# Prompt attention of three branches: one phase, two heads in step, values on column halves

## The reference

```python
h = einsum('bsd,de->bse', x, w_in)              # q, k, v of each branch, ..., gates (3 * 1024 columns)
# A: causal, logits + F[t] - F[s]; B: window of 128 with learned sinks, 2 key heads for 8 heads;
# C: keys of 96, causal by chunks of 64
s = einsum('bqhd,bkhd->bhqk', q, k);  s = where(mask, s, -inf)
o = einsum('bhqk,bkhd->bqhd', softmax(s), v)    # B: the sink joins the sum of the softmax
br_n = o_n * silu(gate_n)                       # stored as br_n
merged = sum_n sigmoid(g_n) * (br_n @ w_br_n);  y = merged @ w_o
```

## Time and profile before

| | us |
|---|---|
| median of 3 runs | 3792.36 (3791.45 to 3795.2) |
| the profiled execution | 3789.74 |
| its span, first to last instruction | 3788.1 |
| PE busy in the span | 3390.3 (89%), 20866 matmuls |
| DVE, ACT, POOL busy | 1411.7, 885.1, 125.5 |
| mean granted clock of TensorE | 0.952 of full speed |

### The profile page before, as it was taken

One profiled execution on the slowest core, in us unless ns is written; L12 is line 12 of the kernel. 1 busy time (PEld: TensorE's weight loads), 2 busy tenths in 40 slices (PEclk: granted clock), 3 DMA queues, 4 the chain that ended last, 5 costly groups with the idle time before them and its releaser, 6 DMA issues. The chain is left out here.

```text
span 3788.1 us, 54850 instructions
## 1 busy us (share of the span) xinstructions
PE 3390.3 (89%) x20866; PEld 2834.0 (75%) x20866; DVE 1411.7 (37%) x3261; ACT 885.1 (23%) x1982; POOL 125.5 (3%) x64
## 2 busy tenths in 40 slices
PE   0999978998998997989969999789989999978988
PEld 0888865887997885667758888568879878855877
DVE  5114233333343332354631233334333333323556
ACT  1221212332222332220221112123322233322110
POOL 0000000100100000000000000000000001000000
PEclk9999988999999998989979999889999989988999
DMA  5322225221433225753442222342233243186533
GB/s 194 106 89 94 77 89 160 62 64 39 108 76 98 59 72 142 244 220 126 144 153 92 88 91 67 120 123 64 64 74 91 60 98 87 37 231 212 218 129 107
DMA packets 485460, 423.06 MB, mean 112 GB/s; under 512 B 300452, under 2 KB 394532, under 8 KB 482916
## 3 DMA queue, kind: packets, MB, share of 16 engines
q1 hardware_dynamic: 451444, 381.06, 33.7%
q10 hardware_dynamic: 33840, 39.66, 3.2%
HBM read 295.36 MB, written 127.64 MB: 112 GB/s over the span
## 5 line engine op out<-in xcount | busy, mean ns | idle before, releaser
L351 PE MATMUL proj_acc<-proj_wh,keep_xh 128*128 128x512 f32 (+1 forms) x1296 | 502.1, 387 | 12.5 <-DVE proj_wl L326 12.5
L352 PE MATMUL proj_acc<-proj_wl,keep_xh 128*128 128x512 f32 (+1 forms) x1296 | 500.8, 386 | 0.0
L353 PE MATMUL proj_acc<-proj_wh,keep_xl 128*128 128x512 f32 (+1 forms) x1296 | 500.7, 386 | 0.0
L351 PEld LDWEIGHTS proj_acc<-proj_wh,keep_xh 128*128 128x128 f32 x1296 | 244.5, 189 | 58.4 <-DVE proj_wl L326 13.3
L352 PEld LDWEIGHTS proj_acc<-proj_wl,keep_xh 128*128 128x128 f32 x1296 | 244.6, 189 | 45.7
L353 PEld LDWEIGHTS proj_acc<-proj_wh,keep_xl 128*128 128x128 f32 x1296 | 244.4, 189 | 45.7
L1820 PE MATMUL up_acc<-up_wh,up_bh 128*128 128x512 f32 x432 | 173.1, 401 | 12.8 <-DVE up_wl L1864 12.8
L326 DVE TENSOR_TENSOR proj_wl<-proj_raw,proj_wh 128x512 fp32r<-128x512 f32 (+1 forms) x144 | 96.1, 676 | 210.6 <-ACT proj_wh L321 210.6
L1056 PE MATMUL att_c_gacc<-att_c_gwh,keep_xh 128*128 (+1 forms) x576 | 170.7, 296 | 2.9 <-DVE att_c_gwl L1185 2.9
L1056 PE MATMUL att_b_gacc<-att_b_gwh,keep_xh 128*128 (+1 forms) x576 | 170.7, 296 | 2.3 <-DVE att_b_gwl L1185 2.3
L1056 PE MATMUL att_a_gacc<-att_a_gwh,keep_xh 128*128 (+1 forms) x576 | 169.9, 295 | 1.9 <-DVE att_a_gwl L1185 1.9
(11 more groups left out here) (338 smaller groups left out, 6803.6 us busy)
## 6 DMA issues: line engine op xcount, KB each, us to landing
up_gates<-scratch_gates SPq DMA_DIRECT2D x18, 1536.0 KB, 8.3
proj_raw<-in_w_in SPq DMA_DIRECT2D x48, 512.0 KB, 3.8
str_ka<-in_cache_a_kT SPq DMA_DIRECT2D x16, 1024.0 KB, 9.0
str_va<-in_cache_a_v SPq DMA_DIRECT2D x16, 1024.0 KB, 5.3
scratch_sg<-proj_out SPq DMA_DIRECT2D x54, 256.0 KB, 2.1
up_br<-scratch_br SPq DMA_DIRECT2D x54, 256.0 KB, 8.2
scratch_gates<-att_a_gout SPq DMA_DIRECT2D x24, 384.0 KB, 2.6
scratch_gates<-att_b_gout SPq DMA_DIRECT2D x24, 384.0 KB, 2.7
```

The costliest lines, as they stand in the source:

```text
L351: nc.tensor.matmul(bank, hi, wh[:, u, kt, 0:w], start=kt == 0, stop=False)
L352: nc.tensor.matmul(bank, hi, wl[:, u, kt, 0:w], start=False, stop=False)
L353: mm = nc.tensor.matmul(bank, lo, wh[:, u, kt, 0:w], start=False, stop=kt == KT - 1)
```

## The change

Three calls become one, `prompt_attention(nc, C, T, S, l)`, and the loop over pairs is written out: twelve units (kind, pair) in one list. A unit has 16 sub-steps m; the row tile is a = m // 2 and the head m % 2, so two heads go in step. Sub-step m holds turn m, score m+2 (or the first two of the next unit), on even m a `back`, a fill if m is 0 to 8, from m = 3 on (not 5) one preparation of the next unit, on odd m the values of both heads. What is new in the operations:

- q and k are kept as a high and a low part in fp32r. ScalarE copies a transposed group as the high part, VectorE subtracts it from the same bank as the low part, and only then is the bank free. A score is three fp32r matmuls a chunk of 512.
- Kind a's extra row: F only goes to k; kind b's sink is no longer a matmul, VectorE copies it behind the score into PSUM. Kind b's two heads share one prepared k.
- Values: v (64 columns of a head) is the weight, on one half of the array's columns, and `pt` is moving; the heads' results stand on partition halves of `oo`. VectorE copies them to `ot`, TensorE transposes back (`back`), and VectorE scales and gates both halves.
- The gate weights have one buffer in two halves; GpSimd splits all of them, after the last fill of the unit before. Rows of q and k have two buffers, a head's half each.

```diff
+    fills = [0, 1, 2, 3, 4, 5, 6, 7, 8]
...
+        for m in range(SUBS):
+            order.append(("turn", n, m))
+            if m + 2 < SUBS:
+                order.append(("score", n, m + 2))
...
+            if m in fills:
+                order.append(("fill", n, fills.index(m)))
+            if ahead and m >= 3 and m != 5:
+                order.append(("prep", n + 1, *ahead.pop(0)))
+            if m % 2:
+                order.append(("value", n, m // 2))
...
-                    last = c + cw == w
-                    nc.tensor.matmul(ss[:, s, c:c + cw], lhs, kt[:, u, first + c:first + c + cw],
-                                     start=True, stop=not last)
+                    nc.tensor.matmul(bank, hi, khi, start=True, stop=False)
+                    nc.tensor.matmul(bank, hi, klo, start=False, stop=False)
+                    nc.tensor.matmul(bank, lo, khi, start=False, stop=c + cw < w)
...
-                        for j, t in enumerate(tiles(a)):
-                            mm = nc.tensor.matmul(oo[:, 0:HD], pt[:, s, j * P:(j + 1) * P], v[:, u, t, :],
-                                                  start=j == 0, stop=j == len(tiles(a)) - 1)
+                for j, t in enumerate(tiles):
+                    for u in range(2):
+                        half = slice(u * HD, u * HD + HD)
+                        mm = nc.tensor.matmul(oo[half, 0:P], v[:, n % 2, t, slice(0, HD) if kind == "b" else half],
+                                              pt[:, u, j * P:(j + 1) * P], start=j == 0, stop=j == len(tiles) - 1,
+                                              skip_group_check=True, tile_position=(0, u * HD))
...
+            def back(n, a):
+                g = groups["back", n, a][0]
+                pe.wait_ge(ot_ready, PT * n + a + 1)
+                bank_free(pe, g)
+                nc.tensor.transpose(tr[:, g % 2, 0:P], ot[:, a % 2, :], C["ident"][:]).then_inc(tr_made, 1)
...
+            def prep(n, x, u, half):
+                g = groups["prep", n, x, u, half][0]
+                act.wait_ge(tr_made, g + 1)
+                nc.scalar.activation(prepared((qh, kh), n, x, u, half), tr[0:ROWS[UNITS[n][0]], g % 2, :], ACT.Copy)\
+                    .then_inc(hi_made, 1)
...
+            def prep(n, x, u, half):
+                g = groups["prep", n, x, u, half][0]
+                if x == "k" and half == 0 and UNITS[n][0] == "a":
+                    extra(n, u)
+                dve.wait_ge(hi_made, preps[n, x, u, half] + 1)
+                nc.vector.tensor_tensor(prepared((ql_, kl_), n, x, u, half), tr[0:ROWS[UNITS[n][0]], g % 2, :],
+                                        prepared((qh, kh), n, x, u, half).bitcast(F32), ALU.subtract)\
+                    .then_inc(tr_taken[g % 2], 1)
...
+                    pool.wait_ge(gw_loaded, 16 * (2 * n + half + 1))
+                    if n:
+                        pool.wait_ge(g_made, NT * n)
```

More of the change, by code:

```diff
@@ L1082, in _, with prepared @@
+            for what, *of in order:
+                {"prep": prep, "score": score, "turn": turn, "value": value, "back": back, "fill": fill}[what](*of)
+        def prepared(tiles, n, x, u, half):
+            return tiles["qk".index(x)][0:ROWS[UNITS[n][0]], n % 2, u, 512 * half:512 * half + 512]
         @block.scalar
         def _(act):
[L1084 to L1092 removed]
@@ L1190, in prompt_attention, with groups_all @@
+            dve.wait_ge(sink_loaded, 16)
+            for what, *of in order:
+                if what == "prep":
+                    prep(*of)
+                elif what == "score":
+                    highest(*of)
+                elif what == "turn":
+                    turn(*of)
+                elif what == "value":
+                    value(*of)
+                elif what == "back":
+                    back(*of)
     ph.end()
+def groups_all(groups):
+    return [g for gs in groups.values() for g in gs]
```

608 lines of the change are left out of this document (276 added, 332 removed).

## The result

| | before | changed |
|---|---|---|
| median, range (us) | 3791.67, 3787.88 to 3795.20 (5 runs) | 3818.11, 3808.94 to 3829.06 (5 runs) |
| ratio to before | | 1.0067 (95%: 1.0051 to 1.0083) |
| profiled execution, span (us) | 3789.74, 3788.1 | 3829.06, 3827.4 |
| mean granted clock | 0.952 | 0.932 |
| attention, layer 1 and 2 (us, first to last matmul) | 820.6, 820.7 | 830.5, 836.5 |

The change makes the kernel 0.7% slower; 3742 was forecast, and the time lies outside the range.

The account below looks back on a forecast made before the run. TensorE was taken to bound the attention stage, busy 778.85 of 826.05 us. Pairs and starts gain 36 us a layer, 72 in all, less 24 for the clock: net 48, so 3742 us, range 3680 to 3805.

Parts of the forecast that it names:

- the round through the two-engine copy: Fill-free sub-steps: softmax, ScalarE copy, VectorE subtraction, next turn take 5.25 us; waits 9.5 us a pair (A, C), 5.5 (B).
- The clock: Fill-free sub-steps: TensorE's clock falls in every second pair, 12 falls at 2 us each, 24 us lost.
- A's extra row: A's second key waits for the row VectorE writes late, part of the chain, 1 us beyond it.
- Rival 2: Short clock falls in every pair: 24 falls at 3 us, 72 us instead of 24; 3790, no change; chance 0.13.
- B's pairs: Branch B: TensorE's work 44.8 us plus 5.5 of waits, 50.3 us a pair against 51.6 before.
- A's and C's clean pairs: Branches A and C: TensorE's work 61.6 us plus 9.5 of waits, 71.1 us a pair against 71.6 before.
- rival 5: Values: the two column halves don't overlap, 0.448 us a tile, 96 us more in all; 3838; chance 0.04.
- rivals 1 and 4: Fill-free waits: shorter, 6 and 3 us a pair (3690, chance 0.20), or longer, 14 and 8 (3834, chance 0.08).
- The start: Start of a layer's attention: three phases become one, about 24 us to first turn; 20 us outside pairs instead of 47.
- Rival 3: Sub-steps 9 to 15: clock stays low throughout, 11 us more a pair in A and C; 3910; chance 0.09.
- The three marks of the last section: Signs of being wrong: A's pair below 68 or above 74, clock 0.5 beyond 10 us between pairs, waits for gate weights.
- The likeliest case: The prediction's own case for the whole kernel: net gain 48 us, 3742, own range 3715 to 3770, chance 0.46.

Follow-up runs that it names:

- e7: The changed kernel with the nine fills of A and C in sub-steps 0, 1, 2, 3, 5, 6, 7, 9 and 10; 3801.13 us, ratio 1.0013.
- e6: The changed kernel plus matmuls nobody reads: eight in sub-steps 9 to 13 of A and C, five ahead of B's later values; 3795.75 us, ratio 1.0006.
- e12: The changed kernel with B's queries and keys taken to 65 rows instead of 64, the keys' 65th row zero; 3792.58 us, ratio 0.9986.
- e13: e11 with B's queries and keys taken to 65 rows instead of 64; 3655.65 us, ratio 0.9642.
- e10: e3 with the value products in the form of the kernel before the change and no transposes back; 3841.96 us, ratio 1.0122.
- e2: The changed kernel with the next unit's preparations in sub-steps 1 to 8 instead of 3, 4 and 6 to 11; 3708.65 us, ratio 0.9782.
- e3: The changed kernel with the next unit's preparations in sub-steps 0 to 7, ahead of the back and the fill; 3695.68 us, ratio 0.9752.
- e11: e3 with each transpose back issued one sub-step later, in the odd ones, ahead of the values there; 3669.33 us, ratio 0.9676.

## Why the prediction was wrong

The wait that I took for the main one, the round through the two-engine copy, was right, and so was its size. What failed are the terms around it. The forecast's span was 3740.4; the profile has 3827.4, 87 us more:

1. **The clock, a term mis-sized, and with it A's extra row**: "I take one fall in every second pair, 12, at 2 us each ... 24 us". Against clean pairs (72.1, which e7 shows for A as well; 53.0, the last of B 55.7 by e6) the pairs of the two layers are 25 and 32 us too long: 56, so +32. A's first three pairs hold 31 of it, B's and C's 25. Falls stand in 14 of 24 pairs, and such a pair is up to 9 us longer. In A not all of this is the clock: the prediction had the wait for the extra row as "part of the chain, 1 us beyond it", and it is 2.9 us, 17.6 in six places, since the row is held until GpSimd's subtraction ends. e6 keeps this wait and cuts these falls to 3.4 us; its six pairs of A are still 19 us too long, 12 less than here, and of the 25 us in B and C nothing is left but its own products. So the falls cost 12 + 25 = 37 us at least, where 24 was charged. The other 19, the wait with a fall of 3.4 us behind it, I can't split exactly: at half the clock six falls of 3.4 us can lose 10 us at most, so 9 or more are the wait's. Rival 2 was thus half true. The row to see the falls by stood in the prediction; I gave the swing a price per fall from no row, and read the mean of 0.97, which belongs to an order with fills at both ends of a pair, as if it spoke for one without.
2. **B's pairs, a term mis-sized**: "B 44.8 + 5.5 = 50.3". 53.0 was measured, and 55.7 for the last, of which some 0.8 can be e6's own products: (3 x 2.7 + 5.4) x 2 = 27. I charged the switch of TensorE's form for the values and not for B's 64-row scores. e12 gives 2.1 of the 2.7 back.
3. **The stream attention, a term left out**: unchanged code, 15.7 us more. The clock is low at its beginning, as before the change, and falls again 27 and 44 us later; the first and the last of these stretches, in windows whose columns are as above:

```profile
1484.00:1500.00 16.00, 8.66 (x30) 5.88 (x31) 2.54 (x6) 2.27 (x4) 1.50 (x2) 0.57 1.16 248
...
1528.00:1538.20 10.20, 10.16 (x33) 7.04 (x33) 1.40 (x6) 1.74 (x5) 0.00 (x0) 0.52 0.93 309
```

   In e6 it takes 141.3 and 137.4, in e13 136.3 and 144.9, so it varies by itself, and I can give only part of these 15.7 to the change. What it varies with shows over both stream attentions of all fifteen kernels, from 134.6 to 148.8 us: a straight line through them is 125.1 us and 0.47 for each us at the lower level (21 to 50 us by the clock rows; correlation 0.92). Here that is 82 us low against 55 before, so 13 of the 15.7.
4. **A's and C's clean pairs**: 72.1 for 71.1, seven a layer, 14. The first fp32r product behind transposes in fp32 starts its successor 0.31 to 0.33 us later, not 0.227 (1318.19 to 1318.52 in the timeline); 16 x 0.09 = 1.4 a pair, of which waits hide some.

32 + 27 + 15.7 + 14 = 89, two more than the 87.

Point by point, what held. *Values*: passes of a pair of halves start a median of 0.109 us apart, 20 records in 1.31 us; 0.218 a tile is confirmed, and with it rival 5 falls. *Fp32r of 128 columns*: 0.112 to 0.117, taken 0.115. *The round*: 5.30 for 5.25, with waits of 1.07, 1.11 and 1.29 where 1 to 2 were named, so rivals 1 and 4 fall as the prediction had them; in A one wait of 2.9 lies outside that. *The nine sub-steps with fills*: in C's pair at 1265.16 the first wait for a bank is that at 1307.9, behind the last fill. *Gate weights*: no wait for them anywhere; behind the last fill of B's first pair GpSimd is done 11.1 us later (1020.12 against 1008.98), for a bound of 13, and the next fill comes after 14.3. *The start*:

```profile
643.54 1.97 PE L987 MATMUL att_tr<-keep_ident,att_row 128*65 128x128 f32 x8 [9.56 <-DMA att_row<-scratch_qa]
651.77 1.94 PE L987 MATMUL att_tr<-keep_ident,att_row 128*65 128x128 f32 x8 [6.26 <-DVE att_row L1116]
659.67 1.97 PE L987 MATMUL att_tr<-keep_ident,att_row 128*65 128x128 f32 x8 [5.96 <-DMA att_row<-scratch_qa]
...
667.57 0.47 PE L1020 MATMUL att_tr<-keep_ident,att_p 128*128 128x128 f32 x1
```

The first load is issued at 640.24, so the first turn, at 667.57, comes 27.3 us behind it, where 24 was forecast. ("Where it was 14" is a misreading: in the kernel before the first turn stands at 650.87, 11.2 us behind the first load; at 14 is the first gate matmul.) From the first load to the last matmul some 21 us lie outside the pairs, when the clean ones and what they are too long by are taken off; 20 was forecast, so the gain of the starts came. *Rival 3* (low through the whole stretch) did not come in C; A comes near it only with the old values (e10). The three marks of the last section: A's pair is above 74, the clock is low for 13.7 us between pairs, and TensorE doesn't wait for the gates' weights. Two of three said that I was wrong.

The chances: 0.21 for slower, of which no case named the right sum. The likeliest case was right about the waits but for A's extra row, and wrong about the engine's speed. The deeper error is of order: I took where the preparations stand as given and asked what it costs, but did not ask what else the same chain does, which is to make TensorE's queue thin just where nothing dense follows.

## What to carry to other kernels

A copy out of PSUM that needs two engines in turn belongs beside dense work of TensorE; the same instructions, moved by a few sub-steps, were worth 109 to 122 us (e2, e3), four times what the whole change lost. Where TensorE waits and the profile names no releaser, look in the code for what it waits for, and at that operation's own length: here 0.17 us had become 1.5. When a change takes work off TensorE in a stretch that already waits, charge the granted clock of that stretch and of the stage behind it as terms of their own. Count the rows of every operand against 64 before and after: e11 with 65 rows (e13) is the best version found, 3655.65 us, 3.6% below the kernel before.

## What was not expected of the hardware

- An operand of 64 rows, with no tile asked for, costs 0.175 us going in from full-width transposes and 0.086 us coming out; 65 rows cost nothing of it (e12, e13).
- The first fp32r product of 512 columns behind plain fp32 work takes 0.31 to 0.33 us to its successor, the next 0.23.
- The clock can stay low for 30.7 us with TensorE busy 30.39 of them (e10), so a full queue of instructions alone did not bring it back at once.
- VectorE's extra row (128x8 from SBUF to SBUF) takes 0.17 us alone. In the six places where GpSimd's subtraction (128x1024) was under way it took 1.33 to 1.68 and ended 0.03 us behind it, while VectorE's maximum over PSUM, begun at 799.13 beside GpSimd's cast and the start of its subtraction, took its usual 1.09. Why the one is held is not shown here.
- A microsecond at the lower level goes with 0.28 to 0.35 us of time between executions of one kernel (changed, e10, e12), and with 0.47 in the stream attention.
